# Centred values and mean squares in the retention stage, gates on VectorE, and two weight loads issued by ScalarE

## What is computed

```python
def _retention(q, k, v, g, gn_w, gn_b, cos, sin):
    ...
    inner = jnp.einsum('bnihd,bnjhd->bnhij', qc, kc) * decay
    inner = jnp.einsum('bnhij,bnjhe->bnihe', inner, vc)
    ...
    cross = jnp.einsum('bnihd,nbhde->bnihe', qc, prev_states) * xi[None, None, :, :, None]
    o = (inner + cross).reshape(b, s, h, dv)
    o32 = o.astype(jnp.float32)
    mu = jnp.mean(o32, axis=-1, keepdims=True)
    var = jnp.mean(jnp.square(o32 - mu), axis=-1, keepdims=True)
    o = ((o32 - mu) * lax.rsqrt(var + RET_GN_EPS)).astype(dt).reshape(b, s, RET_WIDTH)
    o = o * gn_w + gn_b
    return jax.nn.silu(g) * o
```

## Time and profile before

| | |
|---|---|
| median of 3 runs | 2638.94 us (2637.67 to 2639.61) |
| the profiled execution's own time | 2640.68 us |
| its span on the core | 2638.8 us |
| TensorE busy | 2540.5 us, 96% |
| VectorE, ScalarE, GpSimd busy | 58%, 41%, 38% |
| first copy of a retention unit (MLA step 7), layer 1 | 377.6 us |
| first transposes of the retention stage, layers 1 and 2 | 535.8 us and 1832.4 us |
| last causal product in the retention stage (L2006), layer 2 | 1883.5 us |

### The profile page before, as it was taken

How to read it: one execution, slowest core, us unless ns; L and a number is a source line. 1 busy time by engine, 2 the same in 40 slices (tenths; PEclk the granted TensorE clock), 3 DMA queues, 4 the chain that set the end, 5 groups by cost and what they waited for, 6 DMA issues and landing times. The chain is left out here.

```text
span 2638.8 us, 43248 instructions
## 1 busy us (share of the span) xinstructions
PE 2540.5 (96%) x13148; PEld 2179.0 (83%) x13148; DVE 1543.5 (58%) x3050; ACT 1091.1 (41%) x2507; POOL 1005.8 (38%) x1149
## 2 busy tenths in 40 slices
PE   6999989999999999999999999999999999999997
PEld 5999977878788888888889998777887888888886
DVE  4667555472655455577757765555637445445786
ACT  4444544362522222344444545444534332223444
POOL 3455422174254544301044554223823544451011
PEclk9999999999999999999999999999999999999998
DMA  5111011023232333473341101012222233327533
GB/s 182 29 34 36 19 38 39 21 72 144 72 108 94 101 114 109 154 288 96 95 130 32 35 20 41 6 39 91 97 80 89 79 115 107 112 83 269 190 96 120
DMA packets 238682, 242.68 MB, mean 92 GB/s; under 512 B 27936, under 2 KB 171040, under 8 KB 238496
## 3 DMA queue, kind: packets, MB, share of 16 engines
q1 hardware_dynamic: 237968, 238.34, 28.1%
q10 hardware_dynamic: 528, 2.10, 0.2%
HBM read 172.75 MB, written 67.63 MB: 91 GB/s over the span
## 5 line engine op out<-in xcount | busy, mean ns | idle before, releaser
L2533 POOL TENSOR_TENSOR fw_a_lo<-fw_a_raw,fw_a_hi 128x512 fp32r<-128x512 f32 x132 | 178.6, 1354 | 455.1 <-DVE fw_s_raw L2105 455.1
L2533 POOL TENSOR_TENSOR fw_s_lo<-fw_s_raw,fw_s_hi 128x512 fp32r<-128x512 f32 x176 | 232.2, 1332 | 55.2 <-ACT fw_s_hi L1583 55.2
L745 PE MATMUL banks<-ht_hi,da_hi 128*128 128x512 f32 x496 | 192.9, 389 | 0.0
L745 PE MATMUL banks<-ht_lo,da_hi 128*128 128x512 f32 x496 | 192.9, 389 | 0.0
L745 PE MATMUL banks<-ht_hi,da_lo 128*128 128x512 f32 x496 | 192.9, 389 | 0.0
L745 PE MATMUL banks<-w_diff_hi,ht_hi 128*128 128x384 f32 x512 | 179.6, 351 | 2.3 <-DVE dv L1816 2.0
L745 PE MATMUL banks<-w_diff_hi,ht_lo 128*128 128x384 f32 x512 | 171.9, 336 | 0.0
L745 PE MATMUL banks<-w_diff_lo,ht_hi 128*128 128x384 f32 x512 | 171.6, 335 | 0.0
L2361 POOL TENSOR_TENSOR qk_rot<-rope_a,rope_b 128x512 f32<-128x512 f32 x64 | 82.5, 1292 | 195.0 <-DVE rope_b L1802 175.7
L1837 DVE TENSOR_REDUCE stats<-banks 128x1 f32<-128x1024 f32 (+3 forms) x192 | 138.6, 749 | 30.0 <-PE banks L970 24.1
L1657 ACT ACTIVATE u_two<-u_two 128x512 f32<-128x512 f32 x42 | 26.6, 632 | 280.0 <-DVE u_two L2216 280.0
(11 more groups left out here) (364 smaller groups left out, 7481.0 us busy)
## 6 DMA issues: line engine op xcount, KB each, us to landing
da_raw<-act_scratch SPq DMA_DIRECT2D x154, 256.0 KB, 2.6
fw_a_raw<-in_w_gate_dram SPq DMA_DIRECT2D x88, 256.0 KB, 3.1
act_scratch<-act_s SPq DMA_DIRECT2D x66, 256.0 KB, 3.0
w_diff_raw<-in_w_in_dram SPq DMA_DIRECT2D x24, 512.0 KB, 6.4
fw_a<-in_w_up_dram SPq DMA_DIRECT2D x44, 256.0 KB, 3.2
fw_a_raw<-in_w_up_dram SPq DMA_DIRECT2D x44, 256.0 KB, 2.9
act_scratch<-act_zero SPq DMA_DIRECT2D x44, 256.0 KB, 2.4
act_scratch<-act_one SPq DMA_DIRECT2D x44, 256.0 KB, 2.8
```

The lines of the kernel that those rows point to most:

```text
L745: mm = pe.matmul(bank, lhsT, rhs, start=first and i == 0, stop=last and i == len(pairs) - 1, skip_group_check=resumes)
L2533: pool.tensor_tensor(w[1][:], w[2][:], w[0][:].bitcast(F32), ALU.subtract).then_inc(S["f_lo"], 1)
```

## The change

The value projections are centred when they leave PSUM. `ret_take_z` becomes four ScalarE instructions: q and k, the two heads' values (scaled, each with a sum over its columns), the gate. VectorE subtracts the mean in place of scaling the values. In `ret_output` each group becomes a split product of three matmuls of 64 columns, which all add into the same 64 columns. ScalarE takes the output from PSUM and squares it, VectorE sums the squares, adds the epsilon term, multiplies by the inverse root and by the gate; GpSimd keeps the inverse root and the two affine products, the latter now in even rounds. The two loads of the MLA stage are issued by ScalarE.

```diff
@@ ScalarE @@
+                def ret_take(n):
+                    m = n // 2
+                    act.wait_ge(S["ro_done"], L * PER["ro_done"] + n + 1)
...
+                    act.activation(r_sum[m % 3][:, n % 2], banks[:, RET_OUT[0]:RET_OUT[1] + 1, 0:RET_DIM], ACT.Copy).then_inc(S["r_take"], 1)
+
+                def ret_squares(m):
...
+                    act.activation(r_square[:], r_sum[m % 3][:], ACT.Square).then_inc(S["r_sq"], 1)

                 def ret_take_z(a):
                     if a in ret_unit_at:
                         n = ret_unit_at[a]
                         act.wait_ge(S["z_done"], L * PER["z_done"] + Z_RET + n + 1)
-                        act.activation(r_z[n][:], banks[:, Z_BANK, :], ACT.Copy).then_inc(S["z_free"], 1)
+                        if n == T - 1:
+                            load_second_pair()
+                        if n == RET_UNITS - 1:
+                            load_first_output_columns()
+                        act.activation(r_z[n][:, 0:2 * P], banks[:, Z_BANK, 0:2 * P], ACT.Copy)
+                        for j in range(2):
+                            v = slice(2 * P + RET_DIM * j, 2 * P + RET_DIM * (j + 1))
+                            act.activation(r_z[n][:, v], banks[:, Z_BANK, v], ACT.Copy, scale=xz[:, n // T, j:j + 1], accum_out=v_sum[:, n, j:j + 1])
+                        act.activation(r_z[n][:, 3 * P:4 * P], banks[:, Z_BANK, 3 * P:4 * P], ACT.Copy).then_inc(S["z_free"], 1)
+
+                def load_second_pair():
+                    columns = w_in[L].rearrange("(k p) n -> p k n", p=P)
+                    for i in range(4):
+                        begin = COL_RET + i * RET_W + P
+                        act.dma_start(w_ret[2][:, :, i * P:(i + 1) * P], columns[:, :, begin:begin + P]).then_inc(S["w_in0"], 16)
+
+                def load_first_output_columns():
+                    act.dma_start(w_o[0][2][:], w_out[L].rearrange("(k p) n -> p k n", p=P)[:, :, 0:512]).then_inc(S["w_in0"], 16)
@@ ScalarE, rounds @@
                 for u in RET_STEPS:
+                    if 0 <= u - 3 < RET_UNITS:
+                        ret_take(u - 3)
...
-                    if 0 <= u - 7 < RET_UNITS:
-                        ret_normed(u - 7)
...
+                    if u % 2 == 0 and 0 <= u // 2 - 2 < RET_UNITS // 2:
+                        ret_squares(u // 2 - 2)
@@ SyncE @@
-                        if h * T + T - 1 - t == 9:
-                            sp.wait_ge(S["z_done"], L * PER["z_done"] + Z_RET + T)
-                            load_ret(1)
-                        if h * T + T - 1 - t == 25:
+                        if h * T + T - 1 - t == 28:
                             sp.wait_ge(S["z_done"], L * PER["z_done"] + Z_UNITS)
-                            load_out(0)
                             arrives(causal[:], causal_dram, "ret_in")
@@ TensorE, ret_output @@
                     for j in range(2):
-                        mm = both_parts(j, r_at_hi[n % 2][:, tokens(j)], r_at_lo[n % 2][:, tokens(j)], rv[n % 5][:, j], True, t == 0)
+                        mm = products(ret_rows(j), split((r_at_hi[n % 2][:, tokens(j)], r_at_lo[n % 2][:, tokens(j)]),
+                                                            (rv[n % 5][:, j, 0, :], rv[n % 5][:, j, 1, :])), last=t == 0)
@@ VectorE @@
-                    dve.tensor_tensor(v, v, xz[:, n // T, 0:2].unsqueeze(2).to_broadcast([P, 2, RET_DIM]), ALU.mult)
+                    dve.scalar_tensor_tensor(v, v_sum[:, n, :].unsqueeze(2).to_broadcast([P, 2, RET_DIM]), -1.0 / RET_DIM, v, ALU.mult, ALU.add)
...
+                def ret_sums(m):
...
+                    dve.tensor_reduce(r_ss[:, m % 2], r_square[:], AX_X, ALU.add).then_inc(S["r_ss"], 1)
...
+                def ret_normed(m):
...
+                    dve.tensor_tensor(r_norm[b][:].rearrange("p i (j d) -> p i j d", j=2), r_sum[m % 3][:],
+                                      r_rs[:, b].unsqueeze(3).to_broadcast([P, 2, 2, RET_DIM]), ALU.mult).then_inc(S["r_on"], 1)
...
+                    if u >= 9 and u % 2 == 1:
+                        ret_gated((u - 9) // 2)
@@ GpSimd, rounds @@
-                    if u >= 9 and u % 2 == 1 and u != RET_UNITS - 1:
-                        ret_finish((u - 9) // 2)
-                    if u == RET_UNITS:
-                        ret_finish((u - 10) // 2)
+                    if u >= 8 and u % 2 == 0 and (u - 8) // 2 < RET_UNITS // 2:
+                        ret_affine((u - 8) // 2)
```

More of the change, by code:

```diff
@@ L425, in hybrid_block_kernel @@
     m_rs = small(2, T)
[L426 to L430, removed]
+    v_sum = small(2 * T, 2)
+    r_ss = small(2, 2, 2)
+    r_rs = small(2, 2, 2)
+    r_ms = small(2, 2, 2)
     minus_half = small(4)
@@ L458, in hybrid_block_kernel, with ret_rows @@
         RET_INNER, RET_STATE, RET_OUT = (0, 1), 7, (2, 3)
+        def ret_rows(j):
+            return banks[:, RET_OUT[j], 0:RET_DIM]
         def tokens(t, n=1):
@@ L624, in _ @@
                 sp.sem_inc(S["passed"], 1)
-                load_out(1)
+                arrives(w_o[1][2][:], w_out[L].rearrange("(k p) n -> p k n", p=P)[:, :, 512:D], "w_in1")
                 sp.wait_ge(S["x_saved1"], L * PER["x_saved1"] + 16)
@@ L1138, in ret_output @@
                             at_ = slice(64 * j, 64 * j + 64)
-                            mm = both_parts(j, rt_hi[n % 3][at_, 0, :], rt_lo[n % 3][at_, 0, :], state[at_, :, at_], False, True)
+                            mm = products(ret_rows(j), split((rt_hi[n % 3][at_, 0, :], rt_lo[n % 3][at_, 0, :]),
+                                                                (state[at_, 0, at_], state[at_, 1, at_])), first=False)
                     mm.then_inc(S["ro_done"], 1)
@@ L2017, in ret_inner @@
                         st.then_inc(S["r_st"], 1)
[L2019 to L2033, removed]
-                    dve.sem_inc(S["passed"], 1)
-                    for j in range(2):
-                        st = dve.bn_aggr(mv[:, m % 2, 2 * i + j, :], bn[:, i, j, :])
-                    st.then_inc(S["r_mv"], 1)
+                def ret_sums(m):
+                    dve.wait_ge(S["r_sq"], L * PER["r_sq"] + m + 1)
+                    if m >= 2:
+                        dve.wait_ge(S["r_ms"], L * PER["r_ms"] + m - 1)
+                    dve.tensor_reduce(r_ss[:, m % 2], r_square[:], AX_X, ALU.add).then_inc(S["r_ss"], 1)
                 def ret_state_low(n):
@@ L2045, in ret_state_low, with ret_mean_squares @@
                                                  ALU.mult, ALU.subtract).then_inc(S["r_stlo"], 1)
-                def ret_offset(m):
+                def ret_mean_squares(m):
+                    b, p = m % 2, 2 * m // T
+                    dve.wait_ge(S["r_ss"], L * PER["r_ss"] + m + 1)
+                    if m >= 2:
+                        dve.wait_ge(S["r_rstd"], L * PER["r_rstd"] + m - 1)
+                    dve.scalar_tensor_tensor(r_ms[:, b], r_ss[:, b], 1.0 / RET_DIM, xz[:, p, 2:4].unsqueeze(1).to_broadcast([P, 2, 2]),
+                                             ALU.mult, ALU.add).then_inc(S["r_ms"], 1)
+                def ret_normed(m):
                     b = m % 2
@@ L2050, in ret_offset, with ret_gated @@
                     if m >= 2:
-                        dve.wait_ge(S["r_on"], L * PER["r_on"] + 2 * (m - 1))
-                    dve.scalar_tensor_tensor(r_nb[:, b, :], mv[:, b, :, 0], -1.0, r_rs[:, b, :], ALU.mult, ALU.mult).then_inc(S["r_nb"], 1)
+                        dve.wait_ge(S["r_mx"], L * PER["r_mx"] + m - 1)
+                    dve.tensor_tensor(r_norm[b][:].rearrange("p i (j d) -> p i j d", j=2), r_sum[m % 3][:],
+                                      r_rs[:, b].unsqueeze(3).to_broadcast([P, 2, 2, RET_DIM]), ALU.mult).then_inc(S["r_on"], 1)
+                def ret_gated(m):
+                    b, p = m % 2, 2 * m // T
+                    dve.wait_ge(S["r_gate"], L * PER["r_gate"] + 2 * m + 2)
+                    dve.wait_ge(S["r_gb"], L * PER["r_gb"] + m + 1)
+                    for i in range(2):
+                        n = 2 * m + i
+                        st = dve.tensor_tensor(mixed_rows[:, n % T, MIX_RET + p * P:MIX_RET + (p + 1) * P], r_norm[b][:, i, :],
+                                               r_z[n][:, 3 * P:4 * P], ALU.mult)
+                    st.then_inc(S["r_mx"], 1)
                 for a in MLA_STEPS:
@@ L2072, in _ @@
                 for u in RET_STEPS:
-                    if 0 <= u - 3 < RET_UNITS:
-                        ret_take(u - 3)
+                    m = u // 2 - 2
+                    if u % 2 == 1 and 0 <= m < RET_UNITS // 2:
+                        ret_sums(m)
                     if u < RET_UNITS:
                         ret_low(u)
+                    if u % 2 == 1 and 0 <= m < RET_UNITS // 2:
+                        ret_mean_squares(m)
                     if 0 <= u - 1 < RET_UNITS:
                         ret_inner(u - 1)
-                    if 0 <= u - 3 < RET_UNITS:
-                        ret_moments(u - 3)
```

(4 more changed lines are left out.)

51 lines of the change are left out of this document (15 added, 36 removed).

## The result

| | before | after |
|---|---|---|
| median | 2638.91 us (2637.67 to 2639.61, 4 runs) | 2685.89 us |
| each run | | 2650.38, 2685.60, 2686.17, 2718.96 us |
| mean granted clock of these runs | | 0.994, 0.979, 0.980, 0.966 |

What follows compares the result with a forecast made beforehand. TensorE was taken to bound the kernel, at its own floor of 3.20 us a retention round plus some waits. 10.1 - 7.1 - 4.8 + 8.0 + 1.7 = +7.9 us on 2638.9 gave 2647 us, range 2635 to 2655 us.

Steps and rivals of the forecast that it cites:

- Output weights by ScalarE: End of the MLA stage: stores no longer queue behind 2 MB, so both stalls and the slow clock go, -4.8 us.
- The closing list: Signs at the prediction's end that would show it right or wrong, including late mixed rows or causal table, counted at nothing.
- Products +10.1: Retention rounds, ret_output: one more weight load per split product, 0.33 us a unit with a state part, +10.1 us in all.
- waits -7.1: Retention rounds: with less statistics and affine work on VectorE and GpSimd, all TensorE waits found there go, -7.1 us.
- The price of 0.33 us a round: Retention rounds with a state part: three added weight loads at 0.11 us each per unit.
- Second pair +8.0: MLA step 15: four weight issues on ScalarE delay its copy of unit 7; TensorE stands 4.0 us, +8.0 in two layers.
- clock +1.7: Behind step 15: one more 4 us stretch at the lower clock, in layer 2, +1.7 us, bounds 0 and 3.4.
- Rival 1: Retention rounds: VectorE sets the pace, so rounds shorten and the added matmuls are hidden; 2631 us, chance 0.12.
- rival 2: Retention rounds: the added matmuls cost nothing because their loads hide; 2637 us, chance 0.16.
- rival 3: MLA step 14: ScalarE issues the four loads quickly, its queue being empty; 2642 us, chance 0.12.
- Rival 4: End of the MLA stage: stores still wait, since both queues feed the same DMA engines; 2652 us, chance 0.08.

Runs made afterwards that it cites:

- e5: Changed kernel with the two affine vectors requested behind the mixed rows instead of ahead of the last three stores: 2651.42 us, ratio to before 1.0048.
- e10: Kernel before with the first half of the output weights issued by ScalarE, causal table three stores later, affine vectors behind the mixed rows: 2632.55 us, ratio 0.9981.
- e7: Kernel before with only the products of ret_output changed to three matmuls of 64 columns, VectorE copying instead of adding parts: 2643.11 us, ratio 1.0018.
- e1: Changed kernel with both weight loads, causal table and affine vectors back at their old places on SyncE: 2646.87 us, ratio 1.0034.
- e4: Kernel before with one added wait: SyncE asks for the mixed rows only after VectorE's first causal product of the stage: 2641.80 us.
- e8: Changed kernel with affine vectors behind the mixed rows and the second pair's weights back on SyncE, output weights still on ScalarE: 2639.25 us, ratio 1.0005.
- e9: Changed kernel with five clock-keeping matmuls of 512 columns ahead of the first mixed block, the mixed rows as late as before: 2652.79 us.
- e13: Changed kernel with twelve more clock-keeping matmuls of 512 columns right behind the first mixed block, in round 5: 2660.76 us.
- e12: Changed kernel with only the second pair's weights back on SyncE, table and vectors still ahead of the last three stores: 2644.24 to 2708.50 us in six runs.

## Why the prediction was wrong

*The step that failed* is in the change part by part, "Output weights by ScalarE": "the stores on SyncE's queue no longer stand behind 2 MB, and the causal table and vectors come three stores later", counted as gain. I never set the moved loads against the transfer behind them. The mixed rows had 0.1 us of slack in layer 2, to be read from two views of before (11.6 us to landing, 1847.11 for the block that needs them). Two things use it up. The table and the vectors now stand ahead of the last stores; with the vectors behind the rows (e5) the mixed rows are asked for 2.95 us behind the first transposes of layer 2, as before (3.0), and the mixed block does not wait. And the stands at the end of the MLA stage that I credited had delayed the rounds, and so covered that transfer. In the changed kernel what is left of the stand and the time to the request add up to the same in both layers, 1.27 + 3.75 and 0.16 + 4.95 us; no run changes this stand by itself. The closing list named "a wait in the first mixed block", as something that would add what I had at nothing, but the sum, the bounds and the rivals had no price for it.

*And its size.* I bounded the clock at 4 us of the lower level for each gap, 3.4 us in all. It was about 35 us for each layer with a hole. Stands of 1 us and of 4 us are followed by little where dense products come next (1.27 us at 536: no window below 1.00; step 15: 0.57 for 4 us at 440, 0.59 and 0.73 in two windows at 1740), and by up to 75 us at 1.2 GHz where rounds of small matmuls come next. I took the price of a gap from one stage into another.

*The other steps.*
- Products +10.1, waits -7.1. The price of 0.33 us a round was right (3.53 against 3.20), and the sum of the two terms, +3.0, was near. It can be compared from the first to the sixteenth transposes of a layer. The kernel before takes 48.07 and 46.31 us there, but 1.1 us of the 48.07 are the slow clock at 536 that I credited elsewhere: e10, with the old rounds and no dip, takes 46.96 and 46.31. Against e10, e5 (47.47 and 47.48) is 1.7 us slower, and the products alone (e7: 48.40 and 48.39) are 3.5 us slower. So the split was wrong: most waits go with the products, and the statistics and affine work give only about 1.8. In whole runs the products alone are +4.7 us (e7) and all changes of the rounds +9.0 us (e1). Of the 9.0, 3.5 us of the profiled execution of e1 lie between the last causal product of layer 1 and the first copy of layer 2, where the clock dipped at 1330 and 1655 us. One or both dips are in the profiled runs of e4, e5, e7 and e10 too, and not in the one of the kernel before, so they don't belong to the changed rounds. How much of the 9.0 is the change stays open.
- Output weights -4.8: measured -5.0 alone (e10), and 7.6 between e1 and e8; both pairs also differ in the place of the table and vectors.
- Second pair +8.0 and clock +1.7: measured 11 to 12. The stands were 3.95 and 3.99 us, as worked out. That the longer issues "wait for room" was my reading; the runs show their length and not what they wait for.
- Rival 1 (VectorE sets the pace) and rival 2 (the matmuls are free) fell by the rounds of 3.53 us, rival 3 by the issues of 3.95 us. Rival 4 (the stores still wait) was half true: GpSimd still waits up to 3.2 us, but the 2 MB can't be all of it: with the vectors behind the rows and the 2 MB still on ScalarE its longest wait in the same place of layer 1 is 1.6 us in e5 and 1.8 in e10.

Without the late rows the changed kernel is at 2651.4 us, inside my range and 4.4 above the forecast. With them it is at 2650, 2685 or 2719, by the number of layers in which the stand is followed by a hole. (For 2685 this is profiled; for the other two it is read from the mean clocks of 0.994 and 0.966.)

The Trainium skill, page "TensorE: Matmul & The Clock Gate", section "HAM oscillation — how this bites in real kernels", describes waits for a DMA behind which TensorE starts its next work at the lower clock, and advises more work before each wait or a larger (padded) matmul. Its waits are longer than the ones here, about 3 to 5 us. The trace agrees that the clock is low behind a wait (0.50 behind 1.07 us). No run here tries the page's cure; with the wait filled (e9) the clock stayed at 1.00, and with dense work behind the wait (e13) it came back to 1.00. That TensorE stays at the lower clock while it is listed busy without a gap, as from 1860 to 1930, is not in that section; there the measurement decides.

## What to carry to other kernels

When loads are reordered, work out the slack of every transfer behind them (issue plus time to landing, against the start of the first instruction that needs it), and see which stand you remove was covering it. Price a stand of TensorE by what follows it: ahead of thin work one microsecond may cost thirty. If a wait can't be avoided, fill it with matmuls rather than repair the clock behind it, and when times come in steps, look at the granted clock before anything else.

## What the runs showed of the hardware

- How long TensorE stood at the first mixed block, and what the clock did: 0.26, 0.28 and 0.66 us, nothing; 0.98, 1.06 and 1.07 us, 0.50 for some 75 us each; 1.47, 1.82, 2.79 and 2.96 us, some 65, 28, 20 and 70 us. The length of the hole does not follow the length of the stand. It ended within the rounds twice, and otherwise after the first unbroken row of output projection products of 512 columns had begun.
- Steps of 32 to 35 us lie between the runs of one kernel (2644, 2678, 2708 in e12), with a mean clock of 0.994, 0.981 and 0.968. As one execution of each kernel was profiled, it is open whether the stand was shorter in the executions of 2644 us or the same stand was not followed by a hole.
- Four DMA issues of 512 KB each held up ScalarE's program for 3.95 us, as long as they did SyncE's (3.92 in e8): in this kernel the time did not depend on which engine issued them.
